# An MLA layer inside a two-block decoder step: right half of the down projection first, keys drained before splits, and output weights split one head later

## The reference, cut to what matters

```python
def mla_mixer(h, cos, sin, w_down, q_a_norm, kv_a_norm, w_uq, w_ukv, q_norm, k_norm, w_o):
    down = h @ w_down                                  # 384 | 256 | 64 columns
    c_q = rmsnorm(down[..., :384], q_a_norm)
    c_kv = rmsnorm(down[..., 384:640], kv_a_norm)
    k_rope = down[..., 640:]
    q = (c_q @ w_uq).reshape(bsz, seq, 8, 192)
    kv = (c_kv @ w_ukv).reshape(bsz, seq, 8, 256)      # 128 of key, 128 of value
    k = rmsnorm(concat([kv[..., :128], k_rope over heads]), k_norm)
    q = rmsnorm(q, q_norm)
    # rotation of the last 64 features of q and k, causal softmax, values, then
    return o @ w_o
```

## Time and profile before

| what | value |
|---|---|
| median of three runs | 1366.46 us (1363.78 to 1366.76) |
| the profiled execution's own time | 1367.0 us |
| its span in the trace | 1365.1 us |
| mean granted clock of TensorE over the span | 0.988 of full speed |
| PE busy, VectorE busy, ScalarE busy | 1301.9, 930.9 and 832.0 us |
| MLA layer in the trace | about 299.7 us (first transpose of its norm) to 407 us |
| fox attention in the trace | about 1049 to 1099 us |

### The profile page before, as it was taken

How to read it: one execution, slowest core, us unless ns; L and a number is a source line. 1 busy time by engine, 2 the same in 40 slices (tenths; PEclk the granted TensorE clock), 3 DMA queues, 4 the chain that set the end, 5 groups by cost and what they waited for, 6 DMA issues and landing times.

```text
span 1365.1 us, 16179 instructions
## 1 busy us (share of the span) xinstructions
PE 1301.9 (95%) x6140; PEld 1081.8 (79%) x6140; DVE 930.9 (68%) x900; ACT 832.0 (61%) x896; POOL 38.1 (3%) x51
## 2 busy tenths in 40 slices
PE   6999999998887999999999999999999997999998
PEld 5888888887766888888888888878777775788887
DVE  4586455446757888888888888888865564555542
ACT  5545444346755787878787878777576455634431
POOL 4001000000001000000000000002000000000000
PEclk9999999999998999999999999999999999999999
DMA  9638755544227999999999999999773241455540
GB/s 310 216 125 275 243 183 176 176 142 145 78 78 275 398 350 406 359 412 354 410 356 410 356 410 356 409 370 379 264 277 124 93 154 62 146 193 182 188 154 31
DMA packets 90201, 342.19 MB, mean 251 GB/s; under 512 B 6236, under 2 KB 14129, under 8 KB 66481
## 3 DMA queue, kind: packets, MB, share of 16 engines
q1 hardware_dynamic: 87312, 330.74, 65.6%
q0 software_dynamic: 2816, 10.67, 2.4%
q10 hardware_dynamic: 16, 0.00, 0.0%
HBM read 334.05 MB, written 11.01 MB: 253 GB/s over the span
## 4 chain that ended last, share of the span: by engine, by line
PE 88%; DVE 5%; ACT 4%; issue 2%; DMA 1%; SPq 0%; ACTq 0%; DVEq 0%
PE bank L1630 27%; PE bank L1632 27%; PE bank L1631 27%; DVE w_lo L356 2%; ACT w_hi L351 2%; PE bank L1956 1%; DMA raw_beside<-in_moe_w_down 1%; PE bank L1730 1%; PE bank L1755 1%; PE bank L1937 0%; PE bank L1713 0%; PE bank L1949 0%; DMA x<-in_x 0%; DVE x L1047 0%; ACT xT_hi L648 0%
## 5 line engine op out<-in xcount | busy, mean ns | idle before, releaser
L356 DVE TENSOR_TENSOR w_lo<-raw,w_hi 128x2048 fp32r<-128x2048 f32 (+2 forms) x244 | 549.5, 2263 | 254.1 <-ACT w_hi L351 252.9
L351 ACT ACTIVATE w_hi<-raw 128x2048 fp32r<-128x2048 f32 (+2 forms) x244 | 461.2, 1897 | 237.1 <-PE bank L1632 224.9
L1630 PE MATMUL bank<-w_hi,xT_hi 128*128 128x512 f32 (+2 forms) x672 | 258.6, 385 | 14.4 <-issue 6.7
L1631 PE MATMUL bank<-w_lo,xT_hi 128*128 128x512 f32 (+2 forms) x672 | 255.5, 380 | 0.0
L1632 PE MATMUL bank<-w_hi,xT_lo 128*128 128x512 f32 (+2 forms) x672 | 255.2, 380 | 0.0
L1630 PE MATMUL bank<-w_hi,gT_hi 128*128 128x512 f32 x512 | 201.0, 393 | 2.7 <-DVE gT_lo L1394 1.4
L1632 PE MATMUL bank<-w_hi,gT_lo 128*128 128x512 f32 x512 | 199.5, 390 | 0.0
L1631 PE MATMUL bank<-w_lo,gT_hi 128*128 128x512 f32 x512 | 199.2, 389 | 0.0
L1630 PEld LDWEIGHTS bank<-w_hi,xT_hi 128*128 128x128 f32 x672 | 128.2, 191 | 39.5 <-issue 8.8
L356 DVE TENSOR_TENSOR w_lo<-raw_beside,w_hi 128x2048 fp32r<-128x2048 f32 x64 | 145.4, 2288 | 9.6 <-ACT w_hi L351 9.5
L1632 PEld LDWEIGHTS bank<-w_hi,xT_lo 128*128 128x128 f32 x672 | 128.1, 191 | 23.5
(11 more groups left out here) (381 smaller groups left out, 1335.1 us busy)
## 6 DMA issues: line engine op xcount, KB each, us to landing
raw<-in_moe_w_gate SPq DMA_DIRECT2D x48, 1024.0 KB, 5.4
raw<-in_moe_w_up SPq DMA_DIRECT2D x48, 1024.0 KB, 7.3
raw_beside<-in_moe_w_down SPq DMA_DIRECT2D x32, 1024.0 KB, 9.1
raw<-in_moe_w_down SPq DMA_DIRECT2D x32, 1024.0 KB, 7.6
raw<-in_w_gate_up SPq DMA_DIRECT2D x22, 1024.0 KB, 5.2
raw_beside<-in_moe_w_gate SPq DMA_DIRECT2D x16, 1024.0 KB, 6.5
raw_beside<-in_moe_w_up SPq DMA_DIRECT2D x16, 1024.0 KB, 6.4
raw<-in_conv_w_in SPq DMA_DIRECT2D x12, 1024.0 KB, 8.0
```

Of the source, the lines that this page charges most:

```text
L351: nc.scalar.activation(w_hi[:, slot, :n], raw_of(i, stream)[:, :n], ACT.Copy).then_inc(stream.high, 1)
L356: nc.vector.tensor_tensor(w_lo[:, slot, :n], raw_of(i, stream)[:, :n], w_hi[:, slot, :n].bitcast(F32), ALU.subtract).then_inc(stream.low, 1)
L1630: mm(dst, a_hi, b_hi, start=start, stop=False)
L1631: mm(dst, a_hi, b_lo, start=False, stop=False)
```

## The change

The chunks of the down projection are loaded and computed right half first; the columns that ScalarE drains into follow. `LATENTS` becomes ((3, 4), (0, 1), (2,)): the key and value latents are turned while PE computes the other (left) half. PE starts the product with `w_ukv` after the first group's low part, and turns the other two groups behind its first 12 matmuls. On ScalarE the first group's high part stands ahead of the splits that stood before it. On VectorE, the four drains of keys and values stand together, the splits of two query chunks behind them; both `scale_keys` stand ahead of the rotations. In all attentions ScalarE's exponentials of the next head stand ahead of the filler. In the MLA attention output chunks 0 to 3 are split on ScalarE in steps 1, 3, 5 and 6 (before 0, 2, 4 and 6), on VectorE in steps 2, 4, 6 and 7 (before 0, 2, 4 and 6).

```diff
--- before.py
+++ after.py
@@ -65,7 +65,7 @@
 FIRST_OVER = FIRST_PUT + PUT_JOBS
 
 
-LATENTS = ((0, 1), (3, 4), (2,))
+LATENTS = ((3, 4), (0, 1), (2,))
 UQ_GROUPS = HEADS // 2
 
 SCORE_BANKS = {"mla": (6, 3), "fox": (6, 1), "mem": (6, 3)}
@@ -137,7 +137,7 @@
             first += tall("conv_in", A["conv_w_in"][0], KD, part * D + half * HALF, HALF)
     first += wide("conv_out", A["conv_w_out"][0], KD)
     first += ffn("ffn1", A["ffn_w_gate"][0], 0, A["ffn_w_up"][0], 0, A["ffn_w_down"][0])
-    for q in range(2):
+    for q in (1, 0):
         w, n = A["mla_w_down"][0], DOWN_COLS // 2
         first += [("mla_down", rows(w, k0, 4, q * n, n), 4, n) for k0 in (0, 4)]
     for q in range(2):
@@ -652,7 +652,7 @@
                         filler(h)
 
                 for i in range(-2, n_heads + 1):
-                    for stage, h in ((turn, i + 2), (copy_turned, i), (value_high, i - 1), (filled, i), (exps, i + 1)):
+                    for stage, h in ((turn, i + 2), (copy_turned, i), (value_high, i - 1), (exps, i + 1), (filled, i)):
                         if 0 <= h < n_heads and not (stage is turn and h < turned):
                             stage(h)
 
@@ -725,11 +725,11 @@
                 for j in range(2):
                     used(w1, i + 2 * j + 1)
                     for t in range(T):
-                        ins = A_(dn[:, t, j * n:(j + 1) * n], bank[2 * j + t][:, :n], ACT.Copy,
+                        ins = A_(dn[:, t, (1 - j) * n:(2 - j) * n], bank[2 * j + t][:, :n], ACT.Copy,
                                  scale=rinv[:, t:t + 1])
                     ins.then_inc(sem("mla_dn"), 1)
+                    latents_high(j)
                     w1.ahead(i + 3)
-                    latents_high(j)
                 latents_high(2)
                 act.wait_ge(sem("mla_dn"), 2)
                 for t in range(T):
@@ -789,7 +789,8 @@
                     .then_inc(sem("mla_qk_root"), 1)
 
                 def split_out(h):
-                    w1.ahead(start_of["mla_out"] + h // 2 - AHEAD)
+                    if h in (1, 3, 5, 6):
+                        w1.ahead(start_of["mla_out"] + h // 2 - AHEAD)
 
                 attention("mla", HEADS, [(0, P), (P, 3 * P)], lambda t, h: M["q_scale"][:, 0, t, h:h + 1], turn,
                           lambda h, o: (o[:, h, :], bank[1][:, :S]), split_out, 1)
@@ -1230,14 +1231,16 @@
                 for c in range(2):
                     for s in range(2):
                         if s == 0:
-                            w1.ahead(start_of["mla_ukv"] + c)
+                            if c == 0:
+                                w1.ahead(start_of["mla_ukv"])
                             dve.wait_ge(sem("mla_kv_first"), c + 1)
                         else:
-                            used(w1, start_of["mla_ukv"] + c)
+                            dve.wait_ge(w1.stream.used, start_of["mla_ukv"] + c + 1)
                         for t in range(T):
                             ins = V.tensor_scalar(kv[:, t, c * D + s * HALF:c * D + (s + 1) * HALF],
                                                   bank[2 * s + t][:, :], M["c_rinv"][:, 2 + t:3 + t], None, ALU.mult)
                         ins.then_inc(sem("mla_kv_done"), 1)
+                w1.ahead(start_of["mla_ukv"] + 1)
                 w1.ahead(start_of["mla_uq"])
 
                 def rotate_queries(pair):
@@ -1254,22 +1257,21 @@
                         ins = V.tensor_tensor(rp[:, t, heads_, :], qr, over_heads(cosT[:, 0, t, :]), ALU.mult)
                     link(ins)
                     ins = V.tensor_tensor(rp[:, :, heads_, :], rp[:, :, heads_, :], turned_, ALU.add)
-                    if pair >= 2:
+                    if pair >= 1:
                         ins.then_inc(sem("mla_heads_ready"), 1)
 
                 def scale_keys(t):
                     rk = M["qk_rinv"][:, t, HEADS:]
                     kh = kv[:, t, :].rearrange("p (h d) -> p h d", h=HEADS)
                     V.tensor_tensor(kh[:, :, :NOPE], kh[:, :, :NOPE], per_feature(rk, NOPE), ALU.mult)
-                    ins = V.tensor_tensor(rp[:, t, HEADS:, :], kr[:, t, :].unsqueeze(1).broadcast_to([P, HEADS, ROPE]),
+                    V.tensor_tensor(rp[:, t, HEADS:, :], kr[:, t, :].unsqueeze(1).broadcast_to([P, HEADS, ROPE]),
                                     per_feature(rk, ROPE), ALU.mult)
-                    if t == T - 1:
-                        ins.then_inc(sem("mla_heads_ready"), 1)
 
                 inverse("mla_qk_root", "mla_qk_rinv", 1, M["qk_rinv"][:, :, HEADS:], M["qk_root"][:, :, HEADS:])
                 for t in range(T):
-                    rotate_queries(t)
                     scale_keys(t)
+                rotate_queries(0)
+                rotate_queries(1)
                 def turn(h):
                     if h % 2:
                         return
@@ -1293,7 +1295,8 @@
                     return V.tensor_tensor(to, best, M["q_scale"][:, 1, :, h], ALU.mult)
 
                 def split_out(h):
-                    w1.ahead(start_of["mla_out"] + h // 2 - AHEAD)
+                    if h in (2, 4, 6, 7):
+                        w1.ahead(start_of["mla_out"] + (h - 1) // 2 - AHEAD)
 
                 attention("mla", HEADS, [(0, P), (P, 3 * P)], opposite, turn,
                           lambda h, o: (o[:, h, :], bank[1][:, :S]), split_out, 1)
@@ -1838,14 +1841,15 @@
                         if (j, c) == (1, 0):
                             pe.wait_ge(sem("mla_dn"), 1)
                             turn_latents(0)
-                pe.wait_ge(sem("mla_dn"), 2)
-                turn_latents(1)
-                turn_latents(2)
                 cth, ctl = M["cT_hi"], M["cT_lo"]
-                pe.wait_ge(sem("mla_c_low"), 2)
+                pe.wait_ge(sem("mla_c_low"), 1)
                 for c in range(2):
                     wh, wl = weights(W1, start_of["mla_ukv"] + c, 0)
                     for s in range(2):
+                        if (c, s) == (0, 1):
+                            pe.wait_ge(sem("mla_dn"), 2)
+                            turn_latents(1)
+                            turn_latents(2)
                         if c:
                             pe.wait_ge(sem("mla_kv_done"), s + 1)
                         for k in range(KKV):
```

## The result

Four runs of the changed kernel gave 1379.01 us (median, 1377.39 to 1381.66) against 1366.61 us before (1363.78 to 1366.84): a ratio of 1.0104, with a 95% interval of 1.0085 to 1.0123. The change makes the kernel slower by about 1%. The forecast of 1383.5 us has the sign right and is 4.5 us too high: it had +17.0 us for a change of +12.4.

What follows compares the result with a forecast made beforehand. The prediction took the kernel to be bound by what PE waits for. Terms of 6.0 (holding the -0.2), 2.5, 4.5 and 4.0 gave +17.0 us on 1367.0, less 0.5 for the median: 1383.5 us, range 1374 to 1389.

Steps and rivals of the forecast that it cites:

- Part 1: Wanted latents: VectorE's queue holds their low part, so PE starts `w_ukv` at 321.7 against 321.88 us, -0.2.
- Part 2: Other latent groups: late transposes delay the first drain, PE idles 5 us, `w_uq` starts +6.0 us later (+4.3 to +7.7).
- the slow stretch I had added: In part 2, half clock expected after 5 us without work, ahead of `w_uq`: another 1.68 us.
- The second rival: Second half of the `w_ukv` product does not wait for the drains; `w_uq` starts 0.7 us earlier, total 1376.8 us; 5%.
- Part 3: MLA attention at full clock: early heads gain, later splits and products stand in series; sum +2.5 us.
- Part 4: Clock in the MLA attention: three slow stretches at 1.5 us behind new waits, +4.5 us, bounds 0 and 6.7.
- Part 5: Fox attention: exponentials ahead of `mixed` delay five steps by 0.8 us each, +4.0 us, bounds +2 and +5.
- The sum: Whole kernel: +17.0 us on the profiled 1367.0 gives 1384.0; median 0.5 lower, so 1383.5 us.

Runs made afterwards that it cites:

- second profile of the changed kernel: The changed kernel run once more without any edit, on another chip: median 1379.92 us, ratio 1.0097.
- later splits alone: Kernel before, with only the output chunks split as late as in the changed kernel, on ScalarE and VectorE: 1374.20 us, ratio 1.0057.
- order alone: Kernel before, with only ScalarE's exponentials moved ahead of its filler in all three attentions: 1377.31 us, ratio 1.0086.
- squares ahead: Changed kernel, attention as before; ScalarE's latent squares and roots ahead of the later high parts, VectorE's inverse and first drain ahead of the later low parts: 1368.58 us.
- first drain ahead: Squares-ahead kernel with the wanted latents' low part early, plus VectorE's first drain and remaining low parts ahead of the next `w_uq` split: 1361.14 us, ratio 0.9970.

## Why the prediction was right, and where it was off

**Part 1** holds. PE was to start `w_ukv` at 321.7 us after one idle piece of 3.4 us; it started at 321.48 after 3.34. That DVE's queue alone held the early latents is shown by the run in which the low part stands ahead: the wait vanished.

**Part 2** holds in its steps: transposes at 325.92 (326.05 predicted), first drain at 333.06 (333.25), PE's second chunk at 334.61 (334.7) after 5.13 us (5), `w_uq` +6.2 (+6.0). From 334.61 to 341.99 are 7.4 us for matmuls that take 5.45 at full clock, which is the slow stretch I had added, at 0.57 in the windows. The run with PE's order put back shows that this order is the cause, as the queues of ACT and DVE stood. That the reordered key scales and rotations cost nothing holds too: from the start of `w_uq` to head 0 it is 20.39 us before and 20.32 after, and 20.31 to 20.37 in the other runs. What I had not seen is that the late scale was one of two things ahead of the drain. The other is the split of 1152 columns. In the changed kernel it ends at 333.1 us, behind the scale of 330.3, and my chain had both in it. That it binds even with the scale early took two runs to find.

**The second rival**, which was the Trainium skill's rule to rotate independent groups through the PSUM banks (Perfetto Trace Analysis, section Optimizing Tensor Performance), would have given 1376.8 us. The groups do rotate here, and PE waited 5.13 us for a bank. With scale and drain early PE loses 0.2 and 0.70 us, so the rule describes the kernel only once the drain itself can run.

**Part 3** holds at full clock: 3.84 us from head 0 to 1 (3.8), 3.45 from 1 to 2 (3.44), 8.35 and 8.34 from 2 to 3 and 4 to 5 (8.2). From 6 to 7 the second profile of the changed kernel has 9.47 us with one slow stretch, in which 12 matmuls took 4.40 us and not the 2.85 that they took there before. That is 7.9 without it, 1.7 over the 6.18 of before, where I had 1.3; its tail of 18.07 us at full clock is 0.5 over that of before (0.8). Its whole attention without the slow stretch is 58.02 - 1.55 = 56.5 us, +2.8 against 53.63, where I had +2.5. That split and product stand in series is shown by the run with later splits alone. That the exponentials ahead of the filler help in that place, and hurt where the splits stood before, I had not worked out: I never looked at the order by itself.

**Part 4** is too low in the first profile and wrong in its pieces. I had counted on three stretches, each behind a wait, at +4.5. The waits of 1.07 and 1.21 us in steps 3 and 5 left the clock up; the slow time lay behind the 3.87 us wait and at the tail, and was longer: 10.79 us instead of 7.9, and 20.78 instead of 18.07, which is +5.6. In the second profile it was +1.6.

**Part 5** holds: +3.7 us of fox distances against +4.0, mostly by the waits that came or grew, 0.79, 1.09, 1.13 and 1.42 us (before none, 0.28, 0.34 and 0.62), and the run with the order alone has it all.

**The sum.** +17.0 was predicted and +14.7 measured on the profiled executions. Terms of 6.0, 7.0 (parts 3 and 4) and 4.0 measured 6.2, 8.4 and 3.7, that is 1.3 more. What failed is the sentence that sums them "on the profiled execution's 1367.0": it keeps every slow stretch of before outside the changed places. Two of them, ahead of fox, did not occur (-3.2), and from the norm behind the attention to the first expert product 0.6 us were won. The rest of the 4.5 us is that the profiled execution was the longest of four: its 1381.66 is 2.7 over the median, while I had taken 0.5 off.

How the loss is divided between the parts is in some measure chance. By the table above, the latents cost 6.4 us in the first profile of the changed kernel and 8.2 in the second, the MLA attention 8.4 and 4.4, fox 3.7 in both; the second execution is 13.6 us over the profiled one of before. The waits are the same in both, the time at half clock is not. So it is the waits that bear out the mechanisms, and the closeness of +6.2 to +6.0 for part 2 is in part luck.

## What to carry to other kernels

Before moving a product behind another, follow the operands of the drain, its scale too, through every queue they pass, and go on asking what stands next in line once the first obstacle is gone. A split that seems to delay its engine may fill a wait that is there anyway: ask what the engine would do in that time if the split were not first. Do not add up edits of one pipelined loop, as each decides what the other hides.

## What I had not expected of the hardware

How much of the difference between two runs of one kernel can be the clock. The stretch from the norm ahead of fox to the first fox head was edited in none of the kernels, and ran in all fourteen profiles (those of the kernel before and the changed one among them). Its length takes three values: 64.8 to 64.9 us in four of them, with a mean clock of 1.00 in the one shown above, 66.4 to 66.5 in seven, and 68.0 to 68.1 in three, the kernel before among these (0.95). A slow stretch there costs 1.6 us. What decides whether none, one or two of them occur is not shown; it need not be an edit, for the kernel before alone ran from 1361.36 to 1370.38 us in one group of 35 runs, at mean granted clocks of 0.991 to 0.987. The Trainium skill says on the page TensorE: Matmul & The Clock Gate, section Part 1, that the same kernel can show different numbers of slow matmuls from run to run; it says so of a kernel's beginning, and here it holds in the middle, after 980 us of work. A comparison of two single profiles can be off by three microseconds for this reason, and only distances at full clock, or medians of many runs, are to be compared.

The length of a gap does not tell whether the clock falls. PE's waits of 1.07 and 1.21 us within 3.3 us left the clock at 1.00 in both profiles of the changed kernel, and in the kernel before 2.20 us in front of head 1 were followed by a mean of 0.86. In the runs with squares ahead and with the first drain ahead, the same wait led to the same 5.11 us to the next head, and in five other runs whose attention is that of before to 3.44 or 3.45 us, the full clock's distance. In those five the time was lost later: from head 7 to the norm they took 19.10 to 19.14 us, and the kernel before 17.56. So a slow stretch that one profile shows behind a gap can stand elsewhere in the next, and the attention as a whole is no shorter for it (53.52 to 53.63 us in seven of these eight profiles; with the squares ahead it is 56.25, with time lost in both places). What decides where it falls stays open.
